# Sample-state updates as stacked 32-row matmuls, with a new order of the updates, in a two-layer hybrid decoder step

## The reference

```python
SEQ, DEC_BATCH, DEC_SEQ, DEPTH = 256, 8, 8, 2        # one prompt of 256 tokens, 8 samples of 8 new tokens
N_RET_HEADS, RET_DK, RET_DV = 4, 256, 512
def step(r, inp):                                     # one chunk of retention, per head
    qc, kc, vc = inp
    s = jnp.einsum('bihd,bjhd->bhij', qc, kc) * dmat[None]
    inner = jnp.einsum('bhij,bjhe->bihe', s, vc)
    cross = jnp.einsum('bihd,bhde->bihe', qc, r) * q_decay[None, :, :, None]
    r_new = r * chunk_decay[None, :, None, None] + jnp.einsum(
        'bjhd,bjhe->bhde', kc * k_decay[None, :, :, None], vc)
    return r_new, inner + cross
...
    u = ca * jax.nn.sigmoid(cb)                       # GLU rows, input of a causal depthwise convolution, 31 taps
    padded = jnp.concatenate([c0.astype(u.dtype), u], axis=1)
...
    merged = jax.nn.sigmoid(ga + b_ga) * y_ret + jax.nn.sigmoid(gb + b_gb) * y_conv
    x = x + rms_norm(merged @ w_o, g_mix_post)
    h2 = rms_norm(x, g_ffn_pre)
    f = (jax.nn.silu(h2 @ w_ffn_gate) * (h2 @ w_ffn_up)) @ w_ffn_down
    x = x + rms_norm(f, g_ffn_post)
```

## Time and profile before

| | |
|---|---|
| median of 3 runs | 1716.73 us (1715.11 to 1717.14) |
| profiled execution, its time | 1712.29 us |
| its span | 1710.5 us |
| TensorE busy | 1641.5 us, 96% |
| TensorE weight loads busy | 1581.2 us, 92% |
| VectorE busy | 1173.1 us, 69% |
| ScalarE busy | 678.2 us, 40% |
| GpSimd busy | 359.1 us, 21% |
| DMA | 275.8 MB, 161 GB/s |
| mean granted TensorE clock | 0.975 |

### The profile page before, as it was taken

How to read it: one execution, slowest core, us unless ns; L and a number is a source line. 1 busy time by engine, 2 the same in 40 slices (tenths; PEclk the granted TensorE clock), 3 DMA queues, 4 the chain that set the end, 5 groups by cost and what they waited for, 6 DMA issues and landing times.

```text
span 1710.5 us, 29868 instructions
## 1 busy us (share of the span) xinstructions
PE 1641.5 (96%) x10808; PEld 1581.2 (92%) x10808; DVE 1173.1 (69%) x1666; ACT 678.2 (40%) x966; POOL 359.1 (21%) x353
## 2 busy tenths in 40 slices
PE   8987989999989999999989999999998999999997
PEld 7977978999989989999989999999998998999997
DVE  5897894878766657654447978796967675655544
ACT  5321420514445454334344324251525544533433
POOL 0093492121211005950000402121222100000000
PEclk9988986999999999999999999999999999999999
DMA  8523625473544524444434556556454443344443
GB/s 307 194 84 123 234 87 196 149 249 136 200 138 145 175 75 160 147 148 150 158 129 148 181 176 230 185 185 224 160 207 137 136 150 110 121 150 148 148 160 109
DMA packets 73785, 275.80 MB, mean 161 GB/s; under 512 B 8256, under 2 KB 8256, under 8 KB 72640
## 3 DMA queue, kind: packets, MB, share of 16 engines
q1 hardware_dynamic: 52560, 192.17, 34.4%
q0 software_dynamic: 21104, 82.05, 13.4%
HBM read 230.30 MB, written 43.89 MB: 160 GB/s over the span
## 4 chain that ended last, share of the span: by engine, by line
PE 80%; DVE 8%; issue 6%; POOL 3%; DMA 1%; ACT 1%; DVEq 0%; ACTq 0%; POOLq 0%
PE bank L417 21%; PE bank L419 20%; PE bank L418 20%; PE bank L557 5%; DVE acc L1043 3%; PE bank L565 2%; PE bank L566 2%; PE bank L451 1%; PE bank L446 1%; POOL past L265 1%; PE bank L458 1%; PE bank L437 1%; DVE wlo L1008 1%; PE bank L439 1%; PE bank L438 1%
## 5 line engine op out<-in xcount | busy, mean ns | idle before, releaser
L417 PE MATMUL bank<-hhi,whi 128*128 128x320 f32 x2016 | 661.5, 328 | 14.3 <-DVE tmp L1063 5.4
L419 PE MATMUL bank<-hhi,wlo 128*128 128x320 f32 x2016 | 630.4, 313 | 0.0
L418 PE MATMUL bank<-hlo,whi 128*128 128x320 f32 x2016 | 629.9, 312 | 0.0
L1008 DVE TENSOR_TENSOR wlo<-wring,whi 128x1024 fp32r<-128x1024 f32 x363 | 468.6, 1293 | 204.5 <-ACT whi L751 185.5
L417 PEld LDWEIGHTS bank<-hhi,whi 128*128 128x128 f32 x2016 | 385.6, 191 | 29.7 <-issue 15.3
L418 PEld LDWEIGHTS bank<-hlo,whi 128*128 128x128 f32 x2016 | 385.5, 191 | 12.5 <-issue 3.8
L419 PEld LDWEIGHTS bank<-hhi,wlo 128*128 128x128 f32 x2016 | 384.5, 191 | 0.0
L751 ACT ACTIVATE whi<-wring 128x1024 fp32r<-128x1024 f32 x264 | 277.4, 1055 | 231.9 <-PE bank L419 231.9
L1043 DVE SCALAR_TENSOR_TENSOR acc<-up,par,acc 128x256 f32<-128x256 f32 x480 | 269.5, 625 | 0.0
L1074 DVE SCALAR_TENSOR_TENSOR state<-state,con,bank 128x512 f32<-128x512 f32 x128 | 93.7, 744 | 121.6 <-PE bank L566 121.6
L781 ACT ACTIVATE whi<-wring 128x1024 fp32r<-128x1024 f32 x96 | 101.2, 1054 | 177.2 <-PE bank L419 177.2
(11 more groups left out here) (160 smaller groups left out, 2200.8 us busy)
## 6 DMA issues: line engine op xcount, KB each, us to landing
wring<-w SPq DMA_DIRECT2D x364, 512.0 KB, 3.3
state<-r_in POOLq DMA_DIRECT2D x64, 512.0 KB, 5.5
rs_out<-state POOLq DMA_DIRECT2D x64, 512.0 KB, 4.0
rp_out<-pst POOLq DMA_DIRECT2D x8, 512.0 KB, 5.6
us<-c_in POOLq DMA_DIRECT2D x2, 1216.0 KB, 5.8
cs_out<-us POOLq DMA_DIRECT2D x2, 1216.0 KB, 9.2
cp_out<-up POOLq DMA_DIRECT2D x2, 1144.0 KB, 5.6
con<-consts POOLq DMA_DIRECT2D x1, 1420.0 KB, 9.7
```

Source lines behind the costliest of these rows:

```text
L417: pe.matmul(bank[g][:, 0:T], whi[j][:, k, :], hi, start=start and k == 0, stop=False)
L418: pe.matmul(bank[g][:, 0:T], whi[j][:, k, :], lo, start=False, stop=False)
L419: mm = pe.matmul(bank[g][:, 0:T], wlo[j][:, k, :], hi, start=False, stop=stop and k == n - 1)
L1008: return dve.tensor_tensor(dst, value, hi.bitcast(F32), ALU.subtract)
```

## The change

Keys and values of the 64 sample tokens are copied four times over so that each sample has a band of 32 rows (four groups of its 8 tokens), samples 0 to 3 in one 128-row tile and 4 to 7 in a second. A column of signs turns the bands into high and low parts (keys: high, high, low, zero; values: high, low, high, zero), and one 32-row matmul then gives the sum of the three products that two full-height ones gave. Two samples, in two bands, are updated one behind the other: the half d = 0 of both at k = 3, d = 1 of both at k = 7. The store of a state waits for the update in this new order. An extra pair of transposes of values per head goes through the `aux` banks. Beside that: the table with both log and exp is loaded once before each use, with no small activation; `keep_clock` goes from 20 to 12 at two of its four places; the convolution of the old tokens in layer 0 stands ahead of the stores of `up` and `us`; and taps of VectorE move from the GLU stage (4 to 2 per pair) to the heads and the gate stage.

```diff
-AUX_HEAD, AUX_ACT, AUX_DVE = 28, 8, 20
+AUX_HEAD, AUX_ACT, AUX_DVE = 30, 8, 22
-CIN_TAPS = 4
-FIRST_HEAD_TAPS = (2, 2, 2, 2, 2, 1, 1, 1, 1, 1, 1, 2)
-HEAD_TAPS = (4, 0, 3, 0, 4, 3, 3, 3, 1, 0, 0, 0)
-GB_TAPS = (3, 2, 3, 2, 3, 2, 2, 2)
-EARLY_PAST = 18
+CIN_TAPS = 2
+FIRST_HEAD_TAPS = (2, 2, 2, 2, 2, 2, 2, 1, 1, 1, 1, 2)
+HEAD_TAPS = (4, 0, 3, 0, 4, 4, 3, 3, 2, 0, 0, 0)
+GB_TAPS = (4, 2, 3, 2, 3, 3, 3, 3)
...
-                    pool.wait_ge(dve_aux, (l * HEADS + hd) * AUX_DVE + (3 + 2 * b + 2))
+                    pool.wait_ge(dve_aux, (l * HEADS + hd) * AUX_DVE + (5 + b // 2 * 4 + 3 + b % 2))
...
+                if l == 0:
+                    pool.wait_ge(par_loaded, 16)
+                    pool.wait_ge(u_loaded, 16)
+                    past_taps(0, past0, stap, par[:, G_CB:G_CW], par[:, G_CW:NPAR])
                 pool.wait_ge(u_ready, l * 16 + 16)
                 pool.dma_start(cp_out[l], up[:, :, :]).then_inc(u_saved, 16)
-                if l:
-                    pool.wait_ge(sample_conv_step, l * SAMPLE_OPS + PAST_OPS)
+                pool.wait_ge(sample_conv_step, l * SAMPLE_OPS + PAST_OPS)
                 pool.dma_start(cs_out[l], us[:, :, :, :]).then_inc(u_saved, 16)
                 pool.wait_ge(u_saved, l * 32 + 32)
-                if l == 0:
-                    past_of_first(0, EARLY_PAST)
-                    head(l, 0, False)
-                    past_of_first(EARLY_PAST, PAD)
-                    new_taps(l)
...
                     value_rows(2)
+                    pe.wait_ge(dup_ready, H * 6 + 6)
+                    for g in range(2):
+                        aux_free(H, A_VS + g)
+                        for e in range(4):
+                            mm = pe.transpose(aux[(A_VS + g) % 3][:, e * P:(e + 1) * P], vdup[:, e, g, :], ident)
+                        mm.then_inc(aux_done, 1)
...
-                if half == 1:
-                    pos = A_U + 2 * b + d
-                    aux_free(H, pos)
-                    pe.matmul(aux[pos % 3][:, :], kdecs[:, b, d * P:(d + 1) * P], vshi[:, :], start=True, stop=False)
-                    pe.matmul(aux[pos % 3][:, :], kdecs[:, b, d * P:(d + 1) * P], vslo[:, :],
-                              start=False, stop=True).then_inc(aux_done, 1)
+            def late_update(l, hd, pair, d):
+                H = l * HEADS + hd
+                pos = A_U + 4 * pair + 2 * d
+                if pos == A_U:
+                    pe.wait_ge(dve_aux, H * AUX_DVE + 5)
+                aux_free(H, pos)
+                aux_free(H, pos + 1)
+                for i in range(2):
+                    b = 2 * pair + i
+                    row = slice(b % 4 * 32, b % 4 * 32 + 32)
+                    pe.matmul(aux[(pos + i) % 3][:, :], kst[row, b // 4, d * P:(d + 1) * P], vst[row, b // 4, :],
+                              start=True, stop=True).then_inc(aux_done, 1)
...
                 if 1 <= j <= 4:
-                    late_state(l, hd, 2 * (j - 1) + k // 4, k % 4 // 2, k % 2)
+                    late_state(l, hd, 2 * (j - 1) + k % 4 // 2, k // 4, k % 2)
+                    if k % 4 == 3:
+                        late_update(l, hd, j - 1, k // 4)
...
-                keep_clock(20)
+                keep_clock(12)
                 first_units(l, 0, lambda k: h_read(l, k))
...
-            def log_table(l, rs):
-                if not (isinstance(rs, int) and rs == 0):
-                    act.wait_ge(rstd_done, l * RSTDS + rs)
-                act.activation(lnv[:, 0:1], eps[:, 0:1], ACT.Ln).then_inc(log_loaded, 1)
+            def log_exp_table():
+                act.preload_act_table_set("natural_log_exp_and_others")
...
+                act.activation(khs[:, :, :], aux[1][:, :].rearrange("p (g d) -> p g d", g=2), ACT.Copy,
+                               scale=con[:, ds(hd + C_KS, 1)]).then_inc(k_signed, 1)
...
-                dve.tensor_tensor(kdecs[:, :, :], src, own, ALU.mult).then_inc(ks_ready, 1)
+                dve.scalar_tensor_tensor(out=kst[:, :, :], in0=aux[1][:, :].rearrange("p (g d) -> p g d", g=2),
+                                         scalar=con[:, ds(hd + C_KM, 1)], in1=khs[:, :, :].bitcast(F32),
+                                         op0=ALU.mult, op1=ALU.add).then_inc(dve_aux, 1)
...
-                lower(vslo[:, :], aux[(A_V + 2) % 3][:, :], vshi[:, :]).then_inc(dve_aux, 1)
+                for g in range(2):
+                    dve.wait_ge(v_signed, H * 2 + (g + 1))
+                    dve.scalar_tensor_tensor(out=vst[:, g, :], in0=aux[(A_VS + g) % 3][:, :], scalar=col(C_VM, 1),
+                                             in1=vhs[:, g, :].bitcast(F32), op0=ALU.mult, op1=ALU.add).then_inc(dve_aux, 1)
```

More of the change, by code:

```diff
@@ L251, in window, with past_taps @@
                 return buf[:, :, :, t0:t0 + n]
-            def past_taps(l, first, last, past, ptap, bias, weights):
+            def past_taps(l, past, ptap, bias, weights):
                 weights = weights.rearrange("p (n k) -> p n k", n=KT)
-                for k in range(first, last):
+                for k in range(PAD):
                     n = min(DS, PAD - k)
@@ L265, in past_taps @@
                         pool.tensor_tensor(window(past, 0, n), window(past, 0, n), window(ptap, 0, n), ALU.add).then_inc(sample_conv_step, 1)
[L266 to L273, removed]
+                bias = bias.rearrange("p (n b t) -> p n b t", b=1, t=1).to_broadcast([P, KT, DB, DS])
+                pool.wait_ge(sample_conv_step, l * SAMPLE_OPS + PAST_OPS - 1)
+                pool.tensor_tensor(window(us, 0, DS), past[:, :, :, :], bias, ALU.add).then_inc(sample_conv_step, 1)
             def new_taps(l):
@@ L494, in early @@
                     mm.then_inc(aux_done, 1)
-                    pe.wait_ge(dup_ready, H * 2 + 1)
-                    for d in range(2):
-                        mm = pe.transpose(aux[1][:, d * P:(d + 1) * P], kdup[:, d, :], ident)
+                    pe.wait_ge(dup_ready, H * 6 + 2)
+                    for g in range(2):
+                        for d in range(2):
+                            mm = pe.transpose(aux[1][:, g * DK + d * P:g * DK + (d + 1) * P], kdup[:, d, g, :], ident)
                     mm.then_inc(aux_done, 1)
@@ L549, in late_state @@
                 s = b % RING
-                if b == 0 and d == 0 and half == 0:
-                    pe.wait_ge(ks_ready, H + 1)
-                    pe.wait_ge(dve_aux, H * AUX_DVE + 3)
                 if d == 0 and half == 0:
@@ L1067, in rope, with update @@
                 dve.tensor_tensor(qkv[:, 2 * i + 1, :], tmp[:, 2, :], tmp[:, 3, :], ALU.add).then_inc(rope_step, 1)
[L1069 to L1071 removed]
+            def update(l, hd, i):
+                pos = A_U + i
+                b, d = i // 4 * 2 + i % 2, i % 4 // 2
                 dve.wait_ge(aux_done, (l * HEADS + hd) * AUX_HEAD + (pos + 1))
@@ L1151, in head @@
                         for i in range(4):
-                            update(l, hd - 1, 2 * (j - 1) + i // 2, i % 2)
+                            update(l, hd - 1, 4 * (j - 1) + i)
                     conv_taps(l, taps[j])
@@ L1212, in _ @@
                         for i in range(4):
-                            update(l, last, 2 * (n - 1) + i // 2, i % 2)
+                            update(l, last, 4 * (n - 1) + i)
                     conv_taps(l, GB_TAPS[n])
@@ L1347, in constants @@
         c[:, C_KDEC + 2 * h + 1] = np.exp(g * (P - 1 - p)) * scale
-        c[:, C_KROW + h] = np.exp(g * (DS - 1 - p % DS)) * scale
+        row = np.exp(g * (DS - 1 - p % DS)) * scale
+        c[:, C_KS + h], c[:, C_KM + h] = row * np.array([1, 1, -1, 0])[p // DS % 4], row * np.array([0, 0, 1, 0])[p // DS % 4]
         c[:, C_QDEC + 64 * h:C_QDEC + 64 * (h + 1)] = np.exp(g * (p[:64] % DS + 1.0))
         c[:, C_CD + h] = math.exp(g * DS)
-    c[:, C_OWN:C_OWN + DB] = p[:, None] % (DB * DS) // DS == np.arange(DB)
+    c[:, C_VS], c[:, C_VM] = np.array([1, -1, 1, 0])[p // DS % 4], np.array([0, 1, 0, 0])[p // DS % 4]
     c[:, C_ID:C_ID + P] = np.eye(P)
```

101 lines of the change are left out of this document (44 added, 57 removed).

## The result

The changed kernel takes 1832.05 us, median of 4 runs (1831.68 to 1836.24), beside 1715.92 us for the kernel before on the same chip (1713.12 to 1717.14, 4 runs): ratio 1.0685, 95% interval 1.0664 to 1.0706, so 116 us slower. Medians here are of all executions of a kernel; ratios leave out those more than 1.5% above its fastest. The prediction had the sign and both mechanisms, but 49 us and a range that ended at 1820. The profiled execution has a span of 1830.3 us (1710.5 before) and a mean granted clock of 0.911.

A forecast was written before the change was run, and what follows sets the result against it. TensorE bounds the heads' update stretch; in layer 0 it waits for VectorE. Updates -20, transposes +9, waits +72, clock +22, layer 0 -30, tables -10, taps +6 sum to +49 us: 1761 profiled, 1765 median, range 1715 to 1820.

The forecast's parts named there:

- the price of the clock: In the heads, products at about half speed after TensorE's idle times in units 3 and 4: 22 us added, bounds 0 and 40.
- Waits for loads: Before state products in units 3 and 4 of each head, late state loads: 4.5 us twice a head, 72 us added.
- The updates: In the heads, a pair of update matmuls at 0.60 us instead of 0.92: 20 us saved, bounds 3 and 43.
- Hidden in the update stretch: In each head, VectorE's work about even and hidden while a unit (8.3 us after) outlasts it; no cost counted.
- Layer 0: Old-token convolution moved to GpSimd's idle time, so VectorE's taps no longer slow the heads: 30 us gained, bounds 12 and 45.
- Tables: At four norms of each layer, no 1.28 us table load between log and exp, with fewer clock-keeping matmuls: 10 us gained.
- Gate taps: In the gate stage, five more VectorE taps per layer, three in its last units, lengthening glo waits: 6 us added.
- high end: Upper end of the range: 7 us loads and clock (98 + 40), update -10, given as 1829, stopped at 1820.
- Loads in time: Rival: in units 3 and 4 loads land in time or nearly; 1671 us without waits and clock loss; chance 0.15.
- The clock holds: Rival: the load waits in the heads come but the clock does not fall; 1743 us; chance 0.2.
- Layer 0 gains little and loads take longer: Rival: layer 0 gains only 12 us and state loads take a microsecond longer; 1799 us; chance 0.15.
- Nothing drained, the pair overlapped: Rival: a pair's two update matmuls run at once without a drain, 0.25 us a pair; 1743 us; chance 0.1.

The follow-up runs named there:

- run 3: Changed kernel plus 8, 12 and 18 small matmuls before the waits for samples 4, 5 and 7, keeping TensorE at work; 1777.19 us, ratio 1.0368.
- Run 4: Kernel before with only the new order of updates (both samples' d = 0, then d = 1), full-height matmuls; 1826.12 us, ratio 1.0635.
- run 1: Changed kernel with the old sample-by-sample order, one single 32-row matmul per half state at each odd k; median 1796.46 us, runs 1751.98 to 1841.12.
- run 2: Changed kernel with the old sample order, both halves of a sample updated as a pair in one 32-row band; 1686.84 us, ratio 0.9838.
- Run 7: Kernel before with only the one log and exp table and keep_clock at 12 in two places; 1705.13 us, ratio 0.9939.
- run 11: Old order with single 32-row updates, plus a 128-column full-height matmul of ones in every second step, 16 a head; 1838.31 us, ratio 1.0726.
- run 10: Changed kernel with old order and masked full-height updates, plus VectorE's convolution taps moved, mostly to the first unit; 1702.00 us over six executions.
- run 5: Kernel before with one full-height matmul per update instead of two, leaving out the values' low parts; 1697.49 us, ratio 0.9911.
- run 9: Changed kernel with the old order, stacked keys masked per sample and one 128-row matmul per half state; 1678.53 us, ratio 0.9784.
- run 6: Changed kernel with old order and same-band pairs, plus VectorE's taps moved from behind the update stretch into and before it; 1694.89 us over six executions.

## Why the prediction was wrong

**The failed step is the price of the clock.** The prediction said: "There the products ran at about half speed for some 3.5 us, 1.8 us lost", and from it 22 us, bounds 0 and 40. Measured by run 3 and the changed kernel: 96.0 - 86.2 = 9.8 us a head, 78 us in eight, an estimate from one head with the clock up. The two runs as a whole differ by 55 us, with 71 us of half speed and the added matmuls still in run 3, so the clock's price is some 55 to 78 us, either way beyond the upper bound. The size was taken from two short falls outside the update stretch. The fall lasts far longer in the update stretch. The trace of before held such a row too, not among those shown ahead (GpSimd and TensorE in head 1 of layer 0, then its windows):

```profile
241.23 1.10 PE L543 MATMUL bank<-stm,vtok 64*128 64x64 f32 x8
...
254.03 1.13 POOL L294 DMA_DIRECT2D rs_out<-state  x2
...
263.35 0.61 PE L557 MATMUL bank<-qd,state 128*128 128x8 f32 x4 [2.46 <-DMA state<-r_in]
```

```profile
260.00:264.00 4.00, 1.54 (x10) 1.19 (x10) 3.50 (x8) 0.65 (x1) 0.53 (x1) 1.00 0.94 331
264.00:268.00 4.00, 4.00 (x17) 3.81 (x17) 1.50 (x2) 0.00 (x0) 0.53 (x1) 0.53 0.97 338
280.00:284.00 4.00, 4.00 (x17) 3.81 (x17) 3.76 (x7) 0.00 (x0) 0.92 (x2) 0.50 0.65 223
```

A wait of 2.46 us for a load in that same stretch, and then 34 us at half speed with TensorE busy throughout. The next head's products start at 335.92 on this timeline, so the head takes 94.7 us, 17.7 above 77.0, at most 15 of them the clock. At 15 us a head the term would have been near 120 and not 22: too much, since at half clock TensorE also meets the next load later, but the range would have reached past 1832. The lesson is in the choice of row: an idle time's aftermath is to be read where the new idle time will be.

**Waits for loads: right.** Predicted 4.5 us twice a head, 72 in all. Run 4 has 4.51 and 4.36 and 71.7 in all; the changed kernel 56 (TensorE) to 63 (its weight loads), fewer, as is to be expected when TensorE at half clock arrives later. The mechanism (the even sample's load behind a store that waits for a whole unit) is shown by runs 1 and 2, in which the old order has none, and by run 4, in which the new order alone has them all.

**The updates: the pair was cheaper, the saving did not arrive.** Predicted -20 for the updates and +9 for transposes. The pair costs 0.51 to 0.53 and not 0.60, 25 us saved on TensorE's queue. Yet in run 3's clean head waits, updates and transposes make 9.2 us, 74 in all, where the prediction's three terms make 61. The trace accounts for the 1.6 us a head between them. The three steps with the small matmuls take 3.20, 4.03 and 5.75 us where 1.40, 0.89 and 0.89 would do, 9.8 us and not 9.0; and the wait behind the stretch, 0.58 us before, is 1.99 in that head (1.58 in run 2, none in the changed kernel's head shown above, whose stretch is long). Less 0.6 for the cheaper pair, that is the 1.6. "Hidden in the update stretch" held for the stretch and not for what follows it.

**Layer 0: the size right (29 for 30), the reason in part.** The last GLU product is at 95.05 us, predicted near 95. But the prediction laid all 29.2 us lost between heads 0 and 2 on VectorE's slow taps. Of these, 17.7 are head 1's, in which GpSimd's taps end at 254.0: they had held up its queue, two stores of states leave together at 254.03, the load behind them (257.40) lands as TensorE has waited 2.46 us, and the clock falls. Moving the taps ahead frees the queue as well, so the gain came. That the size held although more than half of it had a cause the prediction did not name is luck. Run 7, which leaves the taps where they were, keeps the 94.6 us of that head; run 2 has 77.6.

**Tables: right** (10). **Gate taps:** the waits for glo went from 9.0 to 10.8 us, and in run 2's profiled execution about 3 us remain for everything outside the named terms, 6 predicted (by the medians it would be 5 to 6). The gate stage gets four more taps per layer and not five, a head two and not three, which changes no term.

The sum by these measurements, in the profiled runs: 74 + 78 - 29 - 10 + 3 = 116, of 1830.3 - 1710.5 = 119.8 us. The prediction's sum for its high end is wrong by 9: loads of 7 us, 40 for the clock and 10 for the update, with the other terms, add up to +103, 1820, and not 1829. So the range ended just where its own worst terms did, and left nothing for a term outside its bound.

**The rivals.** Loads in time: no, though run 2 is what that world would be (1687, where 1671 was worked out). The clock holds: the opposite. Layer 0 gains little and loads take longer: no, the loads' median is 5.7 us. Nothing drained, the pair overlapped: half right. It does overlap, but a 32-row update among full-height matmuls costs about 0.3 us more than a full-height one: one 32-row matmul costs 0.51, two in two bands 0.51, two in one band 0.74, one at full height 0.22. The Trainium skill (TensorEngine Tiling (Array Packing), Key Properties) says both, that different tiles work in parallel and that a change of mode drains TensorE; these four numbers agree with both halves, though no run separates a drain from another cost of the 32-row shape.

## What to carry to other kernels

When a change delays the last write of a buffer, follow the queue that stores and reloads it down to the consumer before counting what the arithmetic saves: here a reordering for the sake of packed matmuls cost 110 us by itself. Price a stall with its aftermath, read from a stall in the same instruction stream, not from the idle time alone. And try the plain shape first: zero rows in a full-height matmul (0.22 us) were cheaper than a 32-row tile among full-height matmuls (0.51).

## What the hardware showed that was not expected

- The clock can fall to 1.2 GHz with TensorE busy in every window, and stay for 61 to 65 us (run 1; up to 55 us in run 11). The steps' durations confirm the low clock: 1.67 us for 0.89 in the changed kernel, 1.65 in run 1 (state products at 1104.15 and 1105.80). The Trainium skill (TensorE: Matmul & The Clock Gate, Part 1, Seeing it yourself) warns that clock events in a trace can be unreliable and tells of a clock stuck low for more than 50 us; the events here are borne out by the durations.
- In this stretch a fall often lasts until the stretch ends, whether it began with a wait or not: 37 us in the changed kernel, 34 before, 20 to 24 in run 10. With full-height updates (the kernel before, runs 4, 5, 9 and 10) every fall within a stretch of the profiled executions goes with a wait for a load. With single 32-row updates it came without one in most heads, with the pairs in two bands of run 3 only behind the two waits left. With same-band pairs it came in no head of run 2 and in five of run 6, once without a wait. So neither the shape nor the wait alone settles it. Why run 2's pairs hold where run 1's singles do not stays open, as does what makes one head of the same run fall and the next not.
- A delay in GpSimd's queue reaches TensorE's clock: in the kernel before, convolution taps ahead of two stores made a load late, TensorE waited 2.46 us, and 34 us at half speed followed.
